# Projection and retention of a hybrid encoder layer in one stage of two passes

## The chip, the cores and the metric

The kernel runs on one core of a Trainium2 chip. The core has five engines with a queue each: PE (TensorE, matmuls and transposes), DVE (VectorE), ACT (ScalarE), POOL (GpSimd) and SP (SyncE, which here only issues transfers). They run side by side and wait for each other through semaphores. Matmul results go to PSUM, eight banks of 128 x 512 FP32; all else is in SBUF. The metric is the device time of one execution in microseconds (us).

## The reference

The input is 12 tiles of 128 tokens with 1024 columns, in two sequences of 4 and 8 tiles. The part that the change touches computes:

```python
h = _rmsnorm(x, g_mix)
proj = jnp.einsum('bsd,de->bse', h, w_in)            # 1024 -> 512+512+512+512+448
rq, rk, rv, rg, cq, ckv, kr = jnp.split(proj, cuts, axis=-1)
q = _apply_rope(rq...); k = _apply_rope(rk...) * (DK_RET ** -0.5); v = rv...
ret = _retention_bidir(q, k, v, ret_log_decay)       # 8 heads of 64, chunks of 128 tokens
mu = jnp.mean(ret, axis=-1, keepdims=True)
var = jnp.mean(jnp.square(ret - mu), axis=-1, keepdims=True)
ret = ((ret - mu) * lax.rsqrt(var + EPS)).reshape(...) * ret_gn_g
ret_out = jax.nn.silu(rg) * ret
```

Retention of a chunk is `(q k^T * dmat) v` within the chunk, plus `q` times a state that a scan over the chunks carries forward, plus `q` times one that it carries backward. So no chunk's output can be made before the keys and values of its whole sequence are there. Behind this come latent attention, the output projection, a router and 32 gated experts; the change leaves them alone.

## The kernel before

Five stages run one after the other, with a barrier between: `phase_project` (names a_), `phase_retention` (b_), `phase_latent` (c_), the output projection with the router (d_), and the experts (e_). All that the first stage makes goes through the scratch tensor `mid` in DRAM, 12 records of 128 x 3072.

FP32 precision in the large matmuls is had by splitting each operand into a high and a low part and adding three products (`three_passes`, L110 to L112, on tiles of type F32R). The small matmuls of retention are plain FP32; the profile records two instructions for each of them.

`phase_project` holds the whole of w_in, split, in SBUF (`w_hi`, `w_lo`). For each of the 12 tiles PE makes five products with it: C (latents, 448 columns), Q, K, V and G (512 each), each of 8 slices of the contracted dimension with three passes, so 24 matmuls. DVE rotates queries and keys (`rotate`), PE transposes C, Q and K through one bank (`transpose_out`, L248), ACT takes them out, and SP stores the record (L209). While tile t is projected PE also transposes x of tile t + 1 (L225), ACT takes its high part and DVE its low part.

`phase_retention` first loads keys and values of every tile (L484), weighs the values with both decays on DVE (L687), makes the chunk's states with 8 matmuls (L549) and copies them out. Then DVE runs the scan over all chunks. Then, for each tile, SP loads queries, keys, values and gates (L494, L495), PE makes scores (L562, 8 heads, odd and even heads in turn from the two halves of the partitions), products with the states (L572) and outputs (L584), DVE weighs and normalises, POOL multiplies by the gate, PE transposes (L598), ACT copies out, and POOL stores to `mixT` (L531).

`pairs` unrolls the first and the last two tiles and loops over those between.

Of the kernel before, what the change touches and what calls it, by code (L numbers as in the profile page):

```python
# [19 lines left out]
F32 = mybir.dt.float32  # L20
# [8 lines left out]
P = 128  # L29
D = 1024  # L30
# [13 lines left out]
M_QT, M_KT, M_K, M_V, M_G, M_CT = 0, 512, 1024, 1536, 2048, 2560  # L44
M_W = 3072
# [27 lines left out]
def phase_sems(nc, ctx):  # L73

    sems = []

    def clear():
        nc.clear_and_free_semaphores(sems)
        nc.all_engine_barrier()

    ctx.callback(clear)
    return sems


def phase_sem(nc, sems, name):
    sems.append(nc.alloc_semaphore(name))
    return sems[-1]


# [25 lines left out]
def phase_project(nc, x_all, w_in, g_mix, g_q, g_kv, rope, ident_d, mid):  # L115
    with ExitStack() as ctx:
# [8 lines left out]
        w_hi, w_lo = sb("w_hi", [P, KD, D_IN], F32R), sb("w_lo", [P, KD, D_IN], F32R)  # L125
        x_sb = sb("x_sb", [P, 2, D])
        xT_hi, xT_lo = sb("xT_hi", [P, 2, KD, P], F32R), sb("xT_lo", [P, 2, KD, P], F32R)
        rec = sb("rec", [P, M_W])
        rope_sb = sb("rope_sb", [P, 2, 2, DR])
        work = sb("work", [P, 4, 512])  # L130
        part1, part2, q_tok, c_tok = (work[:, i, :] for i in range(4))
        junk = sb("junk", [P, D], BF16)
        g_col = sb("g_col", [P, KD])
        gq_row, gkv_row = sb("gq_row", [P, QRANK]), sb("gkv_row", [P, KVRANK])
        ident = sb("ident", [P, P])
        eps = sb("eps", [P, 1])
        ssq = sb("ssq", [P, 3])
        root = sb("root", [P, 3])
        rstd = sb("rstd", [P, 3])

        stage = [rec[:, i * 1024:(i + 1) * 1024] for i in range(3)]
        stage += [work[:, 2 * i:2 * i + 2, :].rearrange("p a n -> p (a n)") for i in range(2)]
        NST = len(stage)

        pG = [ctx.enter_context(nc.psum_tensor(f"a_pG{g}", [P, 512], F32)) for g in range(5)]
        pX = [ctx.enter_context(nc.psum_tensor(f"a_pX{b}", [P, 512], F32)) for b in range(2)]
        pO = ctx.enter_context(nc.psum_tensor("a_pO", [P, 512], F32))
        C, Q, K, V, G = range(5)
        COLS = {Q: (0, RW), K: (RW, RW), V: (2 * RW, RW), G: (3 * RW, RW), C: (4 * RW, CW)}
        PARTS = KD // 2  # L150

        def part(m):

            c0, w = COLS[m // PARTS]
            k = 2 * (m % PARTS)
            return slice(k, k + 2), slice(c0, c0 + w), stage[m % NST][:, 0:2 * w].rearrange("p (k n) -> p k n", k=2)

        s_const = sem("const")
        s_raw = [sem(f"raw{i}") for i in range(NST)]
        s_whi, s_wlo = sem("whi"), sem("wlo")  # L160
        s_x = [sem("x0"), sem("x1")]
        s_sq = sem("sq")
        s_root, s_rstd = sem("root"), sem("rstd")
        s_croot = sem("croot")
        s_xt = sem("xt")
        s_hi, s_lo = sem("hi"), sem("lo")
        s_proj = sem("proj")
        s_ctok, s_qtok = sem("ctok"), sem("qtok")

        s_ev = {C: s_ctok, Q: s_qtok, K: sem("evk"), V: sem("evv"), G: sem("evg")}  # L170
        s_out = sem("out")
        s_outev = sem("outev")
        s_store = sem("store")
        s_dve = sem("dve")
        s_eps = sem("eps")
# [3 lines left out]
        @block.sync  # L179
        def _(sp):  # L180
            sp.dma_start(x_sb[:, 0, :], x_all[0]).then_inc(s_x[0], 16)
            sp.dma_start(rope_sb[:, 0], rope[0]).then_inc(s_x[0], 16)
            sp.dma_start(ident[:], ident_d).then_inc(s_const, 16)
            sp.dma_start(g_col[:], g_mix.rearrange("(p k) -> p k", k=KD)).then_inc(s_const, 16)
            sp.dma_start(gq_row[:], g_q.partition_broadcast(P)).then_inc(s_const, 16)
            sp.dma_start(gkv_row[:], g_kv.partition_broadcast(P)).then_inc(s_const, 16)
            w_v = w_in.rearrange("(p k) n -> p k n", k=KD)
            for m in range(5 * PARTS):
                k, cols, raw = part(m)
# [4 lines left out]
            def tile(r, half, last):  # L194
                t = 2 * r + half
                if not last:

                    sp.wait_ge(s_xt, 2 * t)
                    sp.wait_ge(s_sq, t)
                    sp.wait_ge(s_ev[K], t)  # L200
                    sp.wait_ge(s_const, 64)
                    sp.dma_start(x_sb[:, 1 - half, :], x_all[t + 1]).then_inc(s_x[1 - half], 16)
                    sp.dma_start(rope_sb[:, 1 - half], rope[t + 1]).then_inc(s_x[1 - half], 16)
                sp.wait_ge(s_outev, 3 * (t + 1))
                sp.wait_ge(s_ev[V], t + 1)
                sp.wait_ge(s_ev[G], t + 1)
                sp.wait_ge(s_ev[K], t + 1)
                sp.wait_ge(s_const, 64)
                sp.dma_start(mid[t], rec[:]).then_inc(s_store, 16)  # L209

            pairs(sp, TILES, tile)
            sp.wait_ge(s_store, 16 * TILES)

        @block.gpsimd
        def _(pool):
            nc.gpsimd.memset(eps[:], EPS).then_inc(s_eps, 1)

        @block.tensor
        def _(pe):
            def transpose_x(n, half):  # L220

                for b in range(2):
                    for j in range(4):
                        k = 4 * b + j
                        ins = pe.transpose(pX[b][:, j * P:(j + 1) * P], x_sb[:, half, k:D:KD], ident[:])  # L225
                    ins.then_inc(s_xt, 1)

            pe.wait_ge(s_const, 64)
            pe.wait_ge(s_x[0], 32)
            transpose_x(0, 0)  # L230

            def project(r, half, g, i):
                t = 2 * r + half
                first = isinstance(t, int) and t == 0
                pe.wait_ge(s_ev[g], t)
                c0, w = COLS[g]
                for k in range(KD):
                    if first and k % 2 == 0:
                        pe.wait_ge(s_wlo, i * PARTS + k // 2 + 1)
                    ins = three_passes(pe, pG[g][:, 0:w], xT_hi[:, half, k, :], xT_lo[:, half, k, :],  # L240
                                       w_hi[:, k, c0:c0 + w], w_lo[:, k, c0:c0 + w], k == 0, k == KD - 1)
                ins.then_inc(s_proj, 1)

            def transpose_out(r, half, i, src):
                t = 2 * r + half
                pe.wait_ge(s_outev, 3 * t + i)
                for j in range(4):
                    ins = pe.transpose(pO[:, j * P:(j + 1) * P], src[:, j * P:(j + 1) * P], ident[:])  # L248
                ins.then_inc(s_out, 1)

            def tile(r, half, last):
                t = 2 * r + half
                first = isinstance(t, int) and t == 0
                pe.wait_ge(s_lo, 2 * (t + 1))
                project(r, half, C, 0)
                project(r, half, Q, 1)
                if first:
                    project(r, half, K, 2)
                    project(r, half, V, 3)
                    project(r, half, G, 4)  # L260
                pe.wait_ge(s_ctok, t + 1)
                transpose_out(r, half, 0, c_tok)
                if not first:
                    project(r, half, K, 2)
                pe.wait_ge(s_qtok, t + 1)
                transpose_out(r, half, 1, q_tok)
                if not first:
                    project(r, half, V, 3)
                pe.wait_ge(s_ev[K], t + 1)
                transpose_out(r, half, 2, rec[:, M_K:M_K + RW])  # L270
                if not last:
                    pe.wait_ge(s_x[1 - half], 32 * (r + 1 + half))
                    transpose_x(t + 1, 1 - half)
                if not first:
                    project(r, half, G, 4)

            pairs(pe, TILES, tile)

        @block.scalar
        def _(act):  # L280
            def hi_of_x(n, half):
                for b in range(2):
                    act.wait_ge(s_xt, 2 * n + b + 1)
                    for j in range(4):
                        k = 4 * b + j
                        ins = nc.scalar.activation(xT_hi[:, half, k, :], pX[b][:, j * P:(j + 1) * P],
                                                   ACT.Copy, scale=g_col[:, k:k + 1])
                    ins.then_inc(s_hi, 1)
# [1771 lines left out]
```

## Time and profile before

| | us |
|---|---|
| median of 3 runs (lowest, highest) | 1807.42 (1805.31, 1809.92) |
| the profiled execution | 1802.13 |
| its span, first to last instruction | 1800.6 |
| busy PE, DVE, ACT, POOL in the span | 1494.7, 1078.9, 835.3, 358.4 |
| mean granted clock of TensorE | 0.908 |

A granted clock of 1.00 is 2.4 GHz and one of 0.50 is 1.2 GHz; a value between is a mix of both over the stretch. Busy PE means that a matmul was under way, at either clock. Start times count from the start of the span.

### The profile page before, as it was taken

Reading aid. Unit: us, or ns where it says so; the run is one execution under the profiler, and the core shown is the slowest. Engines: PE = TensorE matmul, PEld = TensorE weight load, DVE = VectorE, ACT = ScalarE, POOL = GpSimd, SP = SyncE. Lnnn points to the kernel's source line nnn. Section 1 sums busy time; section 2 is a strip of 40 time slices with the busy share of each in tenths; the row PEclk is TensorE's granted clock in tenths of the full one; section 3 lists DMA queues with packets and bytes.
Section 4 is the critical chain, followed back from the end, with each engine's and each line's share of the span. In section 5 each row is a group of like instructions: output and inputs, shape, how many; then the busy total and the mean of one; then the engine's idle time right before and its main releaser. Section 6 shows DMA issues by size and latency. Waiting matters only on the chain. (4 is left out here: it accounts for less than half of the span.)

```text
span 1800.6 us, 21880 instructions
## 1 busy us (share of the span) xinstructions
PE 1494.7 (83%) x7330; PEld 1224.4 (68%) x7330; DVE 1078.9 (60%) x1689; ACT 835.3 (46%) x1139; POOL 358.4 (20%) x327
## 2 busy tenths in 40 slices
PE   6799999954674779996699963999999999999990
PEld 5688888843673657885488852777777777777770
DVE  5322323224774656764345544888788887888784
ACT  5323232321564455543322213776667666766664
POOL 0000000000462000000011213233433433343330
PEclk9899999976675889999699976999999999999995
DMA  7121221224353110001633454999999999999977
GB/s 260 49 97 61 83 83 61 84 81 151 106 175 119 59 65 24 13 12 38 216 116 133 135 215 138 319 359 362 355 355 360 357 361 353 357 361 358 360 234 291
DMA packets 83585, 347.35 MB, mean 193 GB/s; under 512 B 14514, under 2 KB 25922, under 8 KB 57282
## 3 DMA queue, kind: packets, MB, share of 16 engines
q1 hardware_dynamic: 66434, 300.37, 45.6%
q0 software_dynamic: 17104, 46.38, 9.2%
q8 instruction: 26, 0.43, 0.1%
q14 instruction: 21, 0.17, 0.0%
HBM read 288.61 MB, written 63.87 MB: 196 GB/s over the span
## 5 line engine op out<-in xcount | busy, mean ns | idle before, releaser
L1923 DVE TENSOR_TENSOR e_w_lo<-raw,e_w_hi 128x2048 fp32r<-128x2048 f32 x192 | 430.8, 2285 | 40.9 <-ACT e_w_hi L1872 40.9
L1872 ACT CAST e_w_hi<-raw 128x2048 fp32r<-128x2048 f32 x192 | 353.8, 1921 | 0.0
L110 PE MATMUL a_pG<-a_w_hi,a_xT_hi 128*128 128x512 f32 (+1 forms) x480 | 189.8, 395 | 8.7 <-DVE a_w_lo L353 6.1
L112 PE MATMUL a_pG<-a_w_hi,a_xT_lo 128*128 128x512 f32 (+1 forms) x480 | 186.5, 388 | 0.0
L111 PE MATMUL a_pG<-a_w_lo,a_xT_hi 128*128 128x512 f32 (+1 forms) x480 | 186.1, 388 | 0.0
L1772 POOL DMA_INDIRECT e_xg<-s_h_rows,e_who x34 | 84.2, 2477 | 261.3 <-DMA e_who<-s_table 137.9
L110 PE MATMUL e_py<-e_w_hi,e_hT_hi 128*128 128x512 f32 x256 | 104.3, 408 | 30.4 <-DVE e_hT_lo L1955 30.4
L110 PEld LDWEIGHTS a_pG<-a_w_hi,a_xT_hi 128*128 128x128 f32 x480 | 91.2, 190 | 25.9 <-issue 5.5
L110 PE MATMUL e_pg<-e_w_hi,e_xT_hi 128*128 128x512 f32 x256 | 104.3, 408 | 4.9 <-DVE e_w_lo L1923 4.9
L110 PE MATMUL d_po<-d_w_hi,d_mT_hi 128*128 128x512 f32 x192 | 81.7, 426 | 26.0 <-DVE d_w_lo L1552 26.0
L112 PEld LDWEIGHTS a_pG<-a_w_hi,a_xT_lo 128*128 128x128 f32 x480 | 91.1, 190 | 17.2
L111 PEld LDWEIGHTS a_pG<-a_w_lo,a_xT_hi 128*128 128x128 f32 x480 | 91.3, 190 | 15.7
L111 PE MATMUL e_pg<-e_w_lo,e_xT_hi 128*128 128x512 f32 x256 | 101.8, 398 | 0.0
L112 PE MATMUL e_pg<-e_w_hi,e_xT_lo 128*128 128x512 f32 x256 | 101.7, 397 | 0.0
L112 PE MATMUL e_py<-e_w_hi,e_hT_lo 128*128 128x512 f32 x256 | 101.1, 395 | 0.0
L112 PE MATMUL e_pu<-e_w_hi,e_xT_lo 128*128 128x512 f32 x256 | 101.0, 395 | 0.0
L110 PE MATMUL e_pu<-e_w_hi,e_xT_hi 128*128 128x512 f32 x256 | 101.0, 395 | 0.0
L111 PE MATMUL e_pu<-e_w_lo,e_xT_hi 128*128 128x512 f32 x256 | 101.0, 394 | 0.0
L111 PE MATMUL e_py<-e_w_lo,e_hT_hi 128*128 128x512 f32 x256 | 101.0, 394 | 0.0
L1280 DVE TENSOR_TENSOR c_pT_lo<-c_pt,c_pT_hi 128x512 fp32r<-128x512 f32 x80 | 52.1, 684 | 46.8 <-ACT c_pT_hi L1131 46.8
L112 PE MATMUL d_po<-d_w_hi,d_mT_lo 128*128 128x512 f32 x192 | 79.9, 416 | 0.0
L111 PE MATMUL d_po<-d_w_lo,d_mT_hi 128*128 128x512 f32 x192 | 79.9, 416 | 0.0
(314 smaller groups left out, 3092.2 us busy)
## 6 DMA issues: line engine op xcount, KB each, us to landing
raw<-in_w_gate SPq DMA_DIRECT2D x64, 1024.0 KB, 6.6
raw<-in_w_up SPq DMA_DIRECT2D x64, 1024.0 KB, 9.6
raw<-in_w_down SPq DMA_DIRECT2D x64, 1024.0 KB, 8.2
s_mid<-a_rec SPq DMA_DIRECT2D x12, 1536.0 KB
a_x_sb<-in_x SPq DMA_DIRECT2D x12, 512.0 KB, 6.4
b_kv<-s_mid SPq DMA_DIRECT2D x12, 512.0 KB, 4.1
b_qk<-s_mid SPq DMA_DIRECT2D x12, 512.0 KB, 4.1
b_vg<-s_mid SPq DMA_DIRECT2D x12, 512.0 KB, 5.5
```

What stands on the lines that cost most here:

```text
L110: pe.matmul(out, st_hi, mv_hi, start=first, stop=False)
L111: pe.matmul(out, st_hi, mv_lo, start=False, stop=False)
L112: return pe.matmul(out, st_lo, mv_hi, start=False, stop=last)
L1280: nc.vector.tensor_tensor(pT3_lo[:, 4 * i:4 * i + 4, j * P:(j + 1) * P], pt[:, c * 512:(c + 1) * 512].rearrange("p (k i) -> p k i", k=4), ...
L1772: pool.indirect_dma_start(out=xg[half][:], out_offset=None, in_=h_rows, in_offset=bass.IndirectOffsetOnAxis(ap=who[half][:, 0:1], axis=0), ...
L1872: nc.scalar.copy(w_hi[:, j // 2, span(j)], raw[:, j // 2, span(j)]).then_inc(s_whi[j], 1)
L1923: nc.vector.tensor_tensor(w_lo[:, j // 2, span(j)], raw[:, j // 2, span(j)], w_hi[:, j // 2, span(j)].bitcast(F32), ALU.subtract).then_inc ...
```

## The change

`phase_retention` goes, and `phase_project` takes in its work, in two passes over the 12 tiles, without loops (every tile is written out).

Pass 1 makes values and keys. The values are centred over each head's 64 columns (so that the output's mean, which the group norm subtracts, is zero), the keys are rotated, transposed and weighed, and eight matmuls make the chunk's states (`own_state`). Both states of a head stand above each other on the partitions (`st`), and the scan is done step by step between the tiles. Transposed keys and values go to `mid` and come back in pass 2.

Pass 2 loads and transposes x again and makes queries, latents and gates. Between the projections of tile t stand the scores and outputs of tile t - 1 and the transposition of the output of tile t - 2. The queries of a head are written twice side by side, so that one matmul with `st` gives both directions, and it adds to the same bank as the product within the chunk. The weights need not all be in SBUF: three slots hold V, K and Q, and then C and G take the places of V and K. The norm's gain `g_mix` moves from x to the weights. Pieces of the weights are one slice (128 x 512) with six buffers; the first two groups come by SP's queue, the others by POOL's.

The core of the new order, PE's and ACT's:

```diff
+            for t in range(N):
+                pe.wait_ge(s_lo, 2 * (t + 1))
+                if t >= 2:
+                    pe.wait_ge(s_vev, t - 1)
+                project(V, t, pV[t % 2], low)
+                transpose_x(t + 1)
+                project(V, t, pV[t % 2], high).then_inc(s_pv, 1)
+                if t:
+                    own_state(t - 1)
+                if t >= 2:
+                    pe.wait_ge(s_krot, t - 1)
+                project(K, t, pK[t % 2], range(KD)).then_inc(s_pk, 1)
...
+                project(Q, n, pQ, range(KD)).then_inc(s_pq, 1)
+                if t:
+                    scores(t - 1, 0)
+                else:
+                    own_state(N - 1)
...
+                project(C, n, pC, low)
+                if t:
+                    scores(t - 1, 1)
+                project(C, n, pC, high).then_inc(s_pc, 1)
+                if t >= 2:
+                    turn(t - 2)
+                turn_queries(t, 0)
+                if t:
+                    outputs(t - 1)
+                if t + 1 < N:
+                    transpose_x(n + 1)
...
+                project(G, n, pG, low)
+                turn_queries(t, 1)
+                project(G, n, pG, high).then_inc(s_pg, 1)
+                turn_latent(t)
```

```diff
+                if t == 0:
+                    take_keys(N - 1)
+                    take_own(N - 1)
+                    for m in range(G * KD, (G + 1) * KD):
+                        split_w(m)
+                latent_norm(t)
+                if t >= 2:
+                    take_turned(t - 2)
+                take_queries(t, 0)
+                if t:
+                    square_out(t - 1)
+                if t + 1 < N:
+                    hi_of_x(N + t + 1)
+                if t:
+                    root_out(t - 1)
+                take_queries(t, 1)
+                take_gate(t)
+                take_latent(t)
```

```diff
+            def scores(t, odd):
+                rows = slice(odd * DR, (odd + 1) * DR)
+                for pair in range(HR // 2):
+                    cols = slice(pair * P, (pair + 1) * P)
+                    ins = pe.matmul(pS[:, cols], kv[rows, t % 2, cols], qd[rows, 2 * pair + odd, :],
+                                    start=True, stop=True)
+            def outputs(t):
+                for h in range(HR):
+                    out = pO[:, h * DR:(h + 1) * DR]
+                    pe.matmul(out, sc[:, h % 2, h // 2, :], kv[:, t % 2, 512 + h * DR:512 + (h + 1) * DR],
+                              start=True, stop=False)
+                    ins = pe.matmul(out, qs[:, h, :], st[:, t, h, :], start=False, stop=True)
```

ACT's queue before, in the first tile of projection: the latent norm's squares (L313, L315) and roots (L318, L319) and what follows them. `a_pO` is the bank of transposes.

```order
L313 ACTIVATE a_junk,a_ssq<-a_pG0,a_rstd 128x256 [waits a_proj,a_rstd]
L315 ACTIVATE a_junk,a_ssq<-a_pG0,a_rstd 128x128
L318 ACTIVATE a_root<-a_ssq,a_eps 128x1 [waits a_croot]
L319 ACTIVATE a_root<-a_ssq,a_eps 128x1
L301 COPY a_rec<-a_pO 128x512 [waits a_out,a_store]
L301 COPY a_rec<-a_pO 128x512 [waits a_out]
L325 ACTIVATE a_rec<-a_pG3,a_rstd 128x512 [waits a_proj]
```

ACT's queue after the change, in a middle tile of pass 2, from the gate of the tile before to the queries. `a_p6` is the bank of transposes, `a_p2` the latents' and `a_p1` the gates'; L600 is the gate's silu, L573 takes the turned output, L580 the turned queries.

```order
L600 ACTIVATE a_late<-a_p1,a_rstd 128x512 [waits a_pg]
L606 COPY a_ct<-a_p6 128x512 [waits a_cst,a_ct]
L559 ACTIVATE a_c_junk0,a_cssq<-a_p2,a_rstd 128x256 [waits a_cinv,a_pc]
L559 ACTIVATE a_c_junk1,a_cssq<-a_p2,a_rstd 128x128
L563 ACT_TABLE_LOAD
L563 ACTIVATE a_croot<-a_cssq,a_eps 128x1 [waits a_csq]
L564 ACTIVATE a_croot<-a_cssq,a_eps 128x1
L573 COPY a_late<-a_p6 128x512 [waits a_rst,a_rt]
L580 COPY a_qd<-a_p6 128x512 [waits a_qs,a_ps,a_qt]
```

A table load now stands between squares and roots, and the copy that empties the bank of transposes stands behind both.

PE's queue after the change, at the same place: the end of the latent projection (L93 to L95), the output of tile t - 2 turned (L401), the queries turned (L417), and the first outputs of tile t - 1.

```order
L94 MATMUL a_p2<-a_w_lo,a_xT_hi 128x448
L95 MATMUL a_p2<-a_w_hi,a_xT_lo 128x448
L401 MATMUL a_p6<-a_ident,a_late 128x128 [waits a_ctev,a_ret]
L401 MATMUL a_p6<-a_ident,a_late 128x128 x3
L417 MATMUL a_p6<-a_ident,a_tok 128x128 [waits a_rtev,a_qrot]
L417 MATMUL a_p6<-a_ident,a_tok 128x128 x3
L390 MATMUL a_p3<-a_kv,a_late 128x64 [waits a_scan,a_zero,a_nrm,a_qs,a_sc]
L392 MATMUL a_p3<-a_st,a_qs 128x64
```

L417 waits for `a_rtev`, which L573 of ACT gives; before, PE went from one transposition to the next with a whole projection between.

## Rows read from the trace of the kernel before

**Rows 1.** Windows by stage: window, length, busy us (instructions) of each engine, clock, DMA

```profile
60.00:380.00 320.00, 318.96 (x1530) 270.11 (x1528) 95.09 (x278) 82.63 (x231) 0.00 (x0) 0.99 0.20 72
380.00:460.00 80.00, 25.33 (x212) 20.91 (x214) 38.99 (x89) 13.73 (x33) 0.84 (x2) 0.57 0.39 131
460.00:562.50 102.50, 72.63 (x608) 66.76 (x604) 71.38 (x154) 60.90 (x82) 65.49 (x60) 0.72 0.39 134
```

**Rows 2.** Waits of PE, 380 to 563 us: total, times, longest

```profile
PE b_pst L549 <- DVE b_vw L687: 38.8, 11, 20.6
PE b_pin L572 <- ACT b_cur L631: 16.9, 1, 16.9
```

**Rows 3.** Timeline of PE, 354 to 368 us: start, duration, instruction

```profile
354.75 0.36 PE L112 MATMUL a_pG<-a_w_hi,a_xT_lo 128*128 128x448 f32 x1
...
355.36 0.36 PE L112 MATMUL a_pG<-a_w_hi,a_xT_lo 128*128 128x448 f32 x1
...
365.60 0.39 PE L110 MATMUL a_pG<-a_w_hi,a_xT_hi 128*128 128x512 f32 x1
...
366.74 0.39 PE L112 MATMUL a_pG<-a_w_hi,a_xT_lo 128*128 128x512 f32 x1
...
366.97 0.60 PE L248 MATMUL a_pO<-a_ident,a_work 128*128 128x128 f32 x4
...
367.63 0.39 PE L111 MATMUL a_pG<-a_w_lo,a_xT_hi 128*128 128x512 f32 x1
```

**Rows 4.** Timeline of SP, the first and last of nine stores in the loop

```profile
91.01 0.34 SPq L209 DMA_DIRECT2D s_mid<-a_rec  x1
...
322.92 0.36 SPq L209 DMA_DIRECT2D s_mid<-a_rec  x1
```

**Rows 5.** Timeline of PE in retention, at full and (last row) half clock

```profile
491.11 1.90 PE L584 MATMUL b_pno<-b_vg,b_sc 128*128 128x64 f32 x16
494.79 1.16 PE L562 MATMUL b_psc<-b_qk 64*128 64x128 f32 x16 [1.78 <-DMA b_vg<-s_mid]
495.79 1.06 PE L572 MATMUL b_pin<-b_cur,b_qk 64*128 64x128 f32 x16
...
544.49 3.26 PE L584 MATMUL b_pno<-b_vg,b_sc 128*128 128x64 f32 x16 [1.30 <-DVE b_sc L718]
```

**Rows 6.** Timeline of DVE: first and last of the four instructions of one rotation

```profile
361.24 0.75 DVE L364 SCALAR_TENSOR_TENSOR a_work<-a_pG,a_rstd,a_rope_sb 128x512 f32<-128x512 f32 x1 [1.70 <-PE a_pG L112]
...
362.80 0.69 DVE L371 TENSOR_TENSOR a_work<-a_work 128x512 f32<-128x512 f32 x1
```

**Rows 7.** Timeline of ACT: latent norm's first and last, and a table load

```profile
355.82 0.47 ACT L313 ACTIVATE a_junk<-a_pG,a_rstd 128x256 bf16<-128x256 f32 x1 [2.87 <-PE a_pG L112]
...
356.97 0.28 ACT L319 ACTIVATE a_root<-a_ssq,a_eps 128x1 f32<-128x1 f32 x1
...
544.39 1.28 ACT L651 ACT_TABLE_LOAD   x1
```

**Rows 8.** Timeline, 554 to 563 us: the end of retention

```profile
554.39 1.26 POOL L525 TENSOR_TENSOR b_ret<-b_nrm,b_gate 128x512 f32<-128x512 f32 x1
...
556.86 0.58 ACT L657 COPY b_retT<-b_ptr 128x512 f32<-128x512 f32 x1 [3.90 <-PE b_ptr L598]
...
562.68 1.45 SPq L842 DMA_DIRECT2D c_work<-s_mid  x3
```

**Rows 9.** Timeline of PE: the first transposes and the first projection matmul

```profile
8.30 1.97 PE L225 MATMUL a_pX<-a_ident,a_x_sb 128*128 128x128 f32 x8 [8.30 <-DMA a_gkv_row<-in_g_kv]
...
15.36 0.71 PE L110 MATMUL a_pG<-a_w_hi,a_xT_hi 128*128 128x448 f32 x1 [5.08 <-DVE a_w_lo L353]
```

**Rows 10.** Waits of PE (first row) and windows as in rows 1

```profile
PE a_pO L248 <- DVE a_work L395: 3.5, 1, 3.5
...
50.00:55.00 5.00, 2.28 (x10) 1.88 (x11) 3.67 (x7) 1.71 (x4) 0.00 (x0) 0.51 0.00 0
834.00:837.00 3.00, 1.17 (x8) 0.84 (x8) 2.93 (x7) 2.12 (x5) 0.00 (x0) 1.00 0.00 0
```

More of the change, by code:

```diff
@@ L150, in phase_project @@
[L150 to L159, printed above, removed]
+        xT_hi, xT_lo = sb("xT_hi", [P, 2, D], F32R), sb("xT_lo", [P, 2, D], F32R)
+        late = sb("late", [P, NST, 512])
+        st = sb("st", [P, N, HR, DR])
+        wqT = sb("wqT", [P, HR, P])
@@ new lines, in last_of, with first_of @@
+        def last_of(t):
+            return any(t == first + tiles - 1 for first, tiles in SEQS)
+        def first_of(t):
+            return any(t == first for first, _ in SEQS)
+        scan_steps = []
+        for first, tiles in SEQS:
+            for t in range(first, first + tiles):
+                if t > first and not last_of(t):
+                    scan_steps.append((t, slice(0, DR), t, t + 1))
+                if last_of(t):
+                    scan_steps += [(t, slice(DR, P), i + 1, i) for i in range(t - 2, first - 1, -1)]
@@ L177, in phase_project, with states_ready @@
+        TAIL = sum(1 for step in scan_steps if step[0] == N - 1)
+        def states_ready(t):
+            seq_end = next(first + tiles for first, tiles in SEQS if t < first + tiles)
+            return 2 * sum(1 for step in scan_steps if step[0] < seq_end)
         block = ctx.enter_context(nc.Block())
@@ L192, in _ @@
                 sp.dma_start(raw, w_v[:, k, cols]).then_inc(s_raw[m % NST], 16)
[L194 to L209, printed above, removed]
@@ L224, in transpose_x @@
                         k = 4 * b + j
-                        ins = pe.transpose(pX[b][:, j * P:(j + 1) * P], x_sb[:, half, k:D:KD], ident[:])
+                        ins = pe.transpose(pX[b][:, j * P:(j + 1) * P], x_sb[:, n % 2, k:D:KD], ident[:])
                     ins.then_inc(s_xt, 1)
[L228 to L242, printed above, removed]
@@ L279, in _, with hi_of_x @@
+            scores(N - 1, 0)
+            scores(N - 1, 1)
+            turn(N - 2)
+            outputs(N - 1)
+            turn(N - 1)
         @block.scalar
         def _(act):
-            def hi_of_x(n, half):
+            def hi_of_x(n):
                 for b in range(2):
                     act.wait_ge(s_xt, 2 * n + b + 1)
[L284 to L288, printed above, removed]
@@ new lines, in _ @@
+            for m in range(C * KD, (C + 1) * KD):
+                split_w(m)
+            for t in range(N):
+                if t == 0:
+                    turn_keys(N - 1)
+                    weigh_keys(N - 1)
+                    for m in range(G * KD, (G + 1) * KD):
+                        split_w(m)
+                else:
+                    decayed(t - 1, 0)
+                turn_queries(t)
+                if t:
+                    decayed(t - 1, 1)
+                latent(t)
+                weigh_queries(t, 0)
+                if t:
+                    spread(t - 1)
+                if t + 1 < N:
+                    lo_of_x(N + t + 1)
+                if t:
+                    normalise(t - 1)
+                weigh_queries(t, 1)
+                if t < TAIL // 2:
+                    scan(N - 1, t)
@@ L758 @@
+            decayed(N - 1, 0)
+            decayed(N - 1, 1)
+            spread(N - 1)
+            normalise(N - 1)
 W_QN, W_KT, W_VT, W_QR, W_CAT = 0, 1024, 1536, 2048, 2560
```

1056 lines of the change are left out of this document (570 added, 486 removed).

## Prediction

> **What bounds the kernel now.** I read the stages first. In the row for 60 to 380 us of [rows 1] PE is busy 318.96 of 320 us at a granted clock of 0.99: projection is bound by TensorE and nothing else. The two rows after it are retention: from 380 to 460 us PE is busy 25.33 of 80 us, from 460 to 562.5 us 72.63 of 102.5, at clocks 0.57 and 0.72. The waits in [rows 2] name why: PE stood 38.8 us waiting for the weighed values, and 16.9 us once, while the scan of states ran. So retention is 183 us in which TensorE has little to do, and every matmul in it is small. The change puts this work between projection matmuls. The question is what TensorE's own work costs per tile, and which new waits stand in it.
>
> **What a tile costs TensorE, from rows.** In [rows 3] five 512-column matmuls take 366.74 - 365.60 = 1.14 us, 0.228 each; three 448-column ones 0.61, 0.203 each; and between 366.74 and 367.63 stand two 512-column matmuls and four transposes, so a transpose costs (0.89 - 0.456)/4 = 0.11. Test: a projection tile of before is 24 x (4 x 0.228 + 0.203) + 20 x 0.11 = 28.96 us, and the stores in [rows 4] come every (322.92 - 91.01)/8 = 28.99. A group of eight FP32 matmuls with 128 x 128 weights and 64 columns takes 1.90 us at full clock and 3.26 at half, and the eight score matmuls 1.16, after 1.00 of which the next group starts [rows 5].
>
> **Pass 1, per tile.** Values and keys 48 x 0.228 = 10.9, 12 transposes 1.3, eight state matmuls 1.9 (the form of L584: 128 x 128 weights, 64 columns): 14.1 us. DVE has one rotation (363.49 - 361.24 = 2.25 us [rows 6]) and eight to ten operations of 0.69, about 9 us; ACT about 6. Both are covered. If a cover failed, the keys' rotation must be done 6.8 us after their projection, and it needs 2.3.
>
> **Pass 2, per tile.** Queries and gates 10.9, latents 24 x 0.203 = 4.9, 24 transposes 2.6, outputs 16 matmuls of L584's form 3.8. The scores now come as four of one row half and then four of the other, where before they alternated. Bounds: 1.0 as before, 1.9 as L584's; no row shows the grouped form, and I take the middle, 1.5. Together 23.7 us. The Trainium skill, TensorEngine Tiling (Array Packing), Key Properties, says that tiles in different row halves run in parallel, for up to 2x; by that rule grouping them loses it, the price would be 1.9 to 2.0, and the sum 5 to 6 us longer. DVE has some 12 us of work here, ACT some 9, POOL 3.
>
> **The new wait.** PSUM bank a_p6 takes all transposes. In the ACT order the copy that empties it of the retention output (L573) stands behind the latent norm (L559 to L564), which waits for the end of the latent projection and now has a table load in its middle. PE turns that output at once after the latent projection and then needs the bank again for the queries. From [rows 7]: first square to end of second root is 357.25 - 355.82 = 1.43 us, the table load is 1.28, the copy that follows 0.58 [rows 8], the semaphores 0.2: 3.5 us, less the 0.44 that PE uses for its four transposes. So PE stands 3.0 us in each of the ten tiles from the third on: 30 us of the gain go here. Behind PE's wait are the output matmuls, the next x transposes and the gates; nothing else is late, as the other engines have slack. The Trainium skill, ScalarE: Activation LUTs, gives about 2.7 us for a table load; the trace has 1.28 and that is used. By the page's figure the ten waits would be 14 us longer.
>
> **The rest of the path.** Start: the first transposes begin at 8.30 and the first projection matmul at 15.36 [rows 9]. ACT sets the end of tile 0: about 1.2 after the transposes begin a table load of 1.28, four x casts and sixteen weight pieces of 512 elements at 0.58 (11.6), two squares of 1024 elements with roots (at twice 0.58 and 0.3 each, 3), a second table load: 8.3 + 1.2 + 1.3 + 11.6 + 3 + 1.3 = 26.7, with DVE's last subtraction 27 us. A first tile of before needs all five weight groups, now two; that gain is inside the sum. Then eleven tiles of 14.1: 155. In the first of them the state matmuls wait for the decay tables: ACT comes to them behind two x casts (their transposes end at 27 + 2.7 + 0.9) and a square, at 33.3. Then come the table load, five exponentials of 8 columns and eight of 128 columns (between 0.2 and 0.4 each, so some 3.7) and DVE's two weighings of 0.69: 39.7. PE is ready at 27 + 5.5 + 0.9 + 0.4 = 33.8. That is 6 us, and 2 for matmuls at half clock behind so long a wait: 8 us. Tile 0 of pass 2: 15.8 of projection, 2.3 of states, 20 transposes 2.2, and a wait. The eight gate pieces are split only after ACT has taken the last state, 9 us into the tile; at 0.69 each on DVE they end at 15 at the earliest, and the last two, whose buffers come free only then, add a transfer (between nothing and 6 us; I take 3). Behind them on DVE is the queries' rotation, 2.9: 21 us, where PE is ready at 12.7. So 8 us, between 5 and 11. Sum 28.4. Tile 1 without the output's transposes: 23.3. Ten tiles of 26.7: 267. End: last scores and products 3, outputs 5 (between 3.8 and 6.5), square 0.6, table load 1.3, root, reciprocal and normalising 1.3: 3.2, and from POOL's last product to the first DMA of the latent stage 562.68 - 554.39 = 8.3 [rows 8]: 19.5. Together 27 + 155 + 8 + 28.4 + 23.3 + 267 + 19.5 = 528, where the trace of before has 562.7. That is 34 us less before the clock.
>
> **The clock.** Each wait of 3 us is followed by small matmuls. What this does to the granted clock no row decides: in [rows 10] it fell to 0.51 in 50 to 55 us after PE had stood 3.5 us, and it is 0.72 on average in retention [rows 1], but in 834 to 837 PE was busy 1.17 of 3 us and kept 1.00. One fall costs 2.7 us if it lasts over the outputs (2 x 3.26 - 2 x 1.90 [rows 5]). I take four falls in ten tiles, 11 us. So the stage ends at about 539 and the gain is 23 us. Later stages are not touched; they start earlier.
>
> The profiled execution took 1802.13 us; 1802.13 - 23 = 1779. It lies 5.3 under the median of the runs, 1807.42. Prediction: 1785 us.
>
> **The rivals.** (a) The clock holds in pass 2: then 34 us are kept, 1774; with scores at 1.0 and no wait for the decay tables, 1762. For it: 834 to 837. Against it: retention's own clock. (b) The weight pieces that now come by POOL's queue are late, at the change of passes and in the start, and cost 15 to 20 us more: 1800 to 1805. For it: six buffers of one piece, each refilled only after it is split; against it: the six first pieces of the latents lie ready long before. (c) The slower side: the clock falls in every tile of pass 2 and comes back only in the gates. Then the outputs cost 2.7 more, twelve transposes 1.3 (twice 0.11 each), and twelve of the gates' 24 matmuls, at twice 0.228, 2.7: 6.7 per tile, 67 in ten tiles against the 34 saved, 33 us slower than before, 1840. It decides from 3.4 us per tile on. (d) The change does not do what it says: the retention pieces are serial in each tile, because some engine's queue puts every tile's chain on the path. The queues speak against it: the chain of tile t is spread over tiles t + 1 and t + 2.
>
> **How the numbers follow.** Forecast (1775 to 1797) 0.45; clock holds (1760 to 1775) 0.25; late weights (1797 to 1812) 0.14; clock falls always, or serial chains (1812 to 1845) 0.16. What a measurement of this kernel can tell from no change is 0.3%, 5.4 us: 1802 to 1813. Faster 0.76, same 0.10, slower 0.14. The range of 8 in 10 runs from 1764 to 1815.
>
> **What would show it.** Right: steps of 14.1 us between values' projections in pass 1; a line of PE waiting for ACT's L573 ten times for about 3 us, the largest wait of the stage; the ACT table load before L563 in front of it; PE waiting once 6 us for the weighed keys and once about 8 us before the first queries' transposes; the latent stage's first DMA near 540 us. Wrong, if the pass 2 tiles are well under 26.7 us with a clock of 1.00 (wait or scores too dear), or above 29 (clock), or if PE's waits in pass 1 are more than that one.

## The result, and the profile after

| | before | after |
|---|---|---|
| median of 4 runs each (lowest, highest), us | 1808.13 (1805.31, 1809.92) | 1839.31 (1833.08, 1849.72) |
| the profiled execution | 1802.13 | 1849.72 |
| mean granted clock in it | 0.908 | 0.905 |
| first DMA of the latent stage in it | 562.68 [rows 8] | 599.20 |

The change makes the kernel slower: the ratio is 1.018, 95% interval 1.013 to 1.0229, so 31 us by the medians. The profiled execution of after is the longest of its four. Of its 47.6 us over the one of before, 36.5 are there when the latent stage begins. The other 11 lie in later stages, whose code is the same. (What is called the latent stage's first DMA here and in the prediction is its first load from `mid`, L985; a load of weights stands 0.4 us ahead of it, before and after.)

Windows by stage of the changed kernel, with the columns of [rows 1]: the start, pass 1, the change of passes, and most of pass 2.

```profile
0.00:60.00 60.00, 38.99 (x162) 32.19 (x163) 26.75 (x47) 27.30 (x53) 3.80 (x12) 0.89 0.53 174
60.00:190.00 130.00, 130.00 (x704) 111.51 (x703) 81.50 (x144) 54.21 (x101) 4.31 (x8) 1.00 0.27 88
190.00:250.00 60.00, 51.23 (x277) 44.14 (x277) 36.87 (x66) 24.55 (x47) 7.28 (x12) 0.94 0.32 109
250.00:500.00 250.00, 226.63 (x1123) 198.16 (x1121) 85.87 (x170) 67.33 (x131) 25.10 (x24) 0.85 0.15 49
```

Pass 1 is what it was meant to be: PE is busy all 130 us at full clock. In pass 2 PE is busy for 227 of 250 us, far more than in the old retention, but the clock is 0.85: for about 30% of the time the array ran at 1.2 GHz. Busy time hides this; only the clock column tells it.

The waits of PE in the stage, 0 to 600 us (total, times, longest), which answer to [rows 2]:

```profile
PE a_p L417 <- ACT a_late L573: 29.2, 10, 2.9
PE a_p L417 <- DVE a_tok L707: 8.1, 1, 8.1
PE a_p L333 <- DMA a_x_sb<-in_x: 7.6, 1, 7.6
PE a_p L358 <- DVE a_qs L725: 5.3, 2, 4.6
```

The first row is the new wait that the prediction named, ten times 2.9 us. The two old waits of 38.8 and 16.9 us are gone. The third row, PE waiting for x of the third tile, is one that the prediction did not have.

Timeline from 296 to 312 us in a middle tile of pass 2 (start, duration, instruction, idle time before it and what ended it). It answers to [rows 5] and [rows 7]:

```profile
296.28 0.60 PE L401 MATMUL a_p<-a_ident,a_late 128*128 128x128 f32 x4
296.48 0.47 ACT L559 ACTIVATE a_c_junk<-a_p,a_rstd 128x256 bf16<-128x256 f32 x1 [12.18 <-PE a_p L95]
...
297.41 1.28 ACT L563 ACT_TABLE_LOAD   x1
...
299.09 0.56 ACT L573 COPY a_late<-a_p 128x512 f32<-128x512 f32 x1
...
299.80 0.63 PE L417 MATMUL a_p<-a_ident,a_tok 128*128 128x128 f32 x4 [2.92 <-ACT a_late L573]
...
300.26 0.33 PE L390 MATMUL a_p<-a_kv,a_late 128*128 128x64 f32 x2
300.43 0.39 PE L392 MATMUL a_p<-a_st,a_qs 128*128 128x64 f32 x2
...
304.60 0.63 PE L390 MATMUL a_p<-a_kv,a_late 128*128 128x64 f32 x2
...
306.30 1.91 PE L333 MATMUL a_p<-a_ident,a_x_sb 128*128 128x128 f32 x8
...
308.44 0.63 PE L94 MATMUL a_p<-a_w_lo,a_xT_hi 128*128 128x512 f32 x1
...
311.82 0.39 PE L94 MATMUL a_p<-a_w_lo,a_xT_hi 128*128 128x512 f32 x1
```

Read it down the ACT rows first: squares, table load, copy. PE has its four transposes done at 296.88, and the next ones start at 299.80, released by that copy. The outputs follow. Their pairs take 0.33 to 0.39 us at first, and 0.63 or 0.64 from 301 us on; a dense matmul takes 0.63 there and 0.39 again at 311.8. The same stretch by windows (the number after the five engines is the clock):

```profile
298.00:300.00 2.00, 0.20 (x2) 0.23 (x3) 0.71 (x3) 1.64 (x4) 0.05 (x1) 1.00 0.00 0
300.00:302.00 2.00, 2.00 (x16) 2.00 (x15) 1.23 (x6) 0.59 (x1) 0.54 (x1) 0.75 0.34 131
302.00:304.00 2.00, 2.00 (x12) 2.00 (x11) 0.00 (x0) 0.00 (x0) 0.00 (x0) 0.50 0.00 0
...
308.00:310.00 2.00, 2.00 (x7) 1.61 (x6) 1.79 (x4) 0.79 (x2) 0.00 (x0) 0.50 0.59 231
310.00:312.00 2.00, 2.00 (x7) 1.58 (x7) 0.40 (x1) 0.00 (x0) 1.27 (x1) 0.69 0.00 0
```

Here the clock falls 1.2 us after the wait is over, while PE is busy without a gap, and stays at 0.50 for some 10 us, through the outputs, the x transposes and the first gates. All ten tiles have such a fall, and in nine it lasts 10 us (in the first 7). It does not always come at this point: in six tiles it comes 1.2 to 1.4 us after PE went on, and in the other four 0.6 us before, while PE still waits. The next tile is one of these. PE goes on at 332.35, its transposes take 1.08 us from the start where the tile above had 0.63, and the clock is under 1.00 before 332 (PE's columns alone):

```profile
332.35 1.08 PE L417 MATMUL a_p<-a_ident,a_tok 128*128 128x128 f32 x4 [2.92 <-ACT a_late L573]
...
328.00:332.00 4.00, 1.42 (x9) 0.97 0.00 0
332.00:336.00 4.00, 3.65 (x18) 0.50 0.17 66
```

SP's stores give the pace, as in [rows 4]: in pass 1 one per tile, and in pass 2 one per tile.

```profile
91.87 0.33 SPq L242 DMA_DIRECT2D s_mid<-a_kv  x1
...
190.48 0.33 SPq L242 DMA_DIRECT2D s_mid<-a_kv  x1
...
253.36 0.32 SPq L287 DMA_DIRECT2D s_mid<-a_ct  x1
...
511.41 0.32 SPq L287 DMA_DIRECT2D s_mid<-a_ct  x1
543.67 32.00 SPq L287 DMA_DIRECT2D s_mid<-a_ct  x2
```

The last row holds the last two stores together. Seven steps of pass 1 take (190.48 - 91.87)/7 = 14.09 us each; nine of pass 2 take (543.67 - 253.36)/9 = 32.3.

### The profile page after: what moved, and what is told of

The parts are those of the page before. It is cut to its first block and busy times, and to the rows that moved or that the text cites. A ratio compares the mean times of both kernels' runs of the same rounds, so it can differ in the third digit from the quotient of the medians.

```text
span 1848.2 us, 21620 instructions
## 1 busy us (share of the span) xinstructions
PE 1576.9 (85%) x7474; PEld 1300.3 (70%) x7474; DVE 1095.9 (59%) x1592; ACT 842.2 (46%) x1114; POOL 342.0 (19%) x325
## 5 line engine op out<-in xcount | busy, mean ns | idle before, releaser
L93 PE MATMUL a_p<-a_w_hi,a_xT_hi 128*128 128x512 f32 (+1 forms) x480 | 200.1, 417 | 4.1 <-DVE a_w_lo L672 4.1
L94 PE MATMUL a_p<-a_w_lo,a_xT_hi 128*128 128x512 f32 (+1 forms) x480 | 189.9, 396 | 0.0
L95 PE MATMUL a_p<-a_w_hi,a_xT_lo 128*128 128x512 f32 (+1 forms) x480 | 189.6, 395 | 0.0
L93 PE MATMUL e_py<-e_w_hi,e_hT_hi 128*128 128x512 f32 x256 | 104.4, 408 | 30.0 <-DVE e_hT_lo L2098 30.0
L93 PEld LDWEIGHTS a_p<-a_w_hi,a_xT_hi 128*128 128x128 f32 x480 | 94.7, 197 | 22.8 <-DVE a_xT_lo L666 3.7
L93 PE MATMUL e_pg<-e_w_hi,e_xT_hi 128*128 128x512 f32 x256 | 104.5, 408 | 4.9 <-DVE e_w_lo L2066 4.9
L95 PEld LDWEIGHTS a_p<-a_w_hi,a_xT_lo 128*128 128x128 f32 x480 | 93.4, 195 | 18.7
L93 PE MATMUL d_po<-d_w_hi,d_mT_hi 128*128 128x512 f32 x192 | 83.6, 435 | 25.7 <-DVE d_w_lo L1695 25.7
L94 PEld LDWEIGHTS a_p<-a_w_lo,a_xT_hi 128*128 128x128 f32 x480 | 94.6, 197 | 15.4
L95 PE MATMUL e_pg<-e_w_hi,e_xT_lo 128*128 128x512 f32 x256 | 101.9, 398 | 0.0
L95 PE MATMUL e_py<-e_w_hi,e_hT_lo 128*128 128x512 f32 x256 | 101.1, 395 | 0.0
L95 PE MATMUL e_pu<-e_w_hi,e_xT_lo 128*128 128x512 f32 x256 | 101.0, 395 | 0.0
L93 PE MATMUL e_pu<-e_w_hi,e_xT_hi 128*128 128x512 f32 x256 | 101.0, 394 | 0.0
L95 PE MATMUL d_po<-d_w_hi,d_mT_lo 128*128 128x512 f32 x192 | 81.4, 424 | 0.0
L93 PEld LDWEIGHTS e_py<-e_w_hi,e_hT_hi 128*128 128x128 f32 x256 | 48.1, 188 | 46.2 <-DVE e_hT_lo L2098 36.3
```

What stands on the lines that cost most here:

```text
L93: pe.matmul(out, st_hi, mv_hi, start=first, stop=False)
L94: pe.matmul(out, st_hi, mv_lo, start=False, stop=False)
L95: return pe.matmul(out, st_lo, mv_hi, start=False, stop=last)
```

## The experiments

Two theories stood against each other at first. W: the wait of 2.9 us, with small matmuls behind it, brings the clock down, and this is the loss. S: the small FP32 matmuls and transposes do it by themselves, with or without the wait. All kernels below are the changed one with an edit, unless said otherwise. "Tile" is the mean step of nine stores in pass 2, "stage" the first DMA of the latent stage in the profiled execution, "falls" the tiles of the ten (the third to the last) in which the clock falls at the wait or behind it, in the profiled execution, "ratio" that to the kernel before on the same chip. The medians are of four executions each, of ten in e3.

| kernel | median us | ratio (95%) | tile us | falls | clock, 250 to 500 us | stage us |
|---|---|---|---|---|---|---|
| after | 1839.31 | 1.018 (1.013 to 1.0229) | 32.3 | 10 | 0.85 | 599.20 |
| e1_turn_early | 1762.05 | 0.9756 (0.9733 to 0.9778) | 24.59 | 0 | 1.00 | 516.78 |
| e2_fill_wait | 1791.66 | 0.9924 (0.99 to 0.9947) | 27.75 | 0 | 1.00 | 550.35 |
| e3_outputs_late | 1806.58 | 1.0007 (0.9989 to 1.0026) | 28.5 | 5 | 0.97 | 556.69 |
| e4_x_first | 1834.88 | 1.0181 (1.0143 to 1.0218) | 31.4 | 9 | 0.88 | 584.62 |
| e5_table_early | 1790.87 | 0.9891 (0.9861 to 0.9922) | 27.7 | 3 | 0.95 | 551.25 |
| e12_short_late | 1781.33 | 0.9864 (0.9838 to 0.9891) | 26.44 | 0 | 1.00 | 539.08 |
| e8_all_fixes | 1754.78 | 0.97 (0.9674 to 0.9726) | 24.59 | 0 | 0.98 | 510.74 |
| e9_scores_in_turn | 1747.21 | 0.9666 (0.9636 to 0.9695) | 23.36 | 0 | 0.99 | 504.16 |
| e10_all | 1740.03 | 0.9614 (0.9586 to 0.9641) | 23.36 | 0 | 0.96 | 494.64 |
| e11_rope_split | 1739.69 | 0.9638 (0.9618 to 0.9657) | 23.36 | 0 | 0.97 | 495.51 |

(In the last four kernels 250 to 500 us reaches past pass 2 or close to its end, so that their clock there is a little under 1.00 for another reason.)

**The wait taken away (e1_turn_early).** PE turns the output of tile t - 2 one half of the latent projection earlier, and ACT takes it before the norm:

```diff
@@ PE @@
-                project(C, n, pC, high).then_inc(s_pc, 1)
                 if t >= 2:
                     turn(t - 2)
+                project(C, n, pC, high).then_inc(s_pc, 1)
@@ ACT @@
-                latent_norm(t)
                 if t >= 2:
                     take_turned(t - 2)
+                latent_norm(t)
```

> Only the order changes: PE turns the output of tile t - 2 before the last 12 matmuls of the latents, and ACT empties the bank of transposes ahead of the latent norm. Theory W (PE's wait of 2.9 us for L573, followed by small matmuls, is what lets the clock fall in each of ten tiles): wait and fall both go, a tile of pass 2 takes 24 to 25 us in place of 32.2, the clock stays at 1.00 there, time 1760 to 1770. Theory S (the stretch of small matmuls lets it fall by itself, with or without the wait): the wait goes, the fall stays, a tile takes about 29.3 us, time about 1810.

The time fell by 77 us against the changed kernel and is 2.4% under before. Window of 250 to 500 us, and ACT's two rows in a middle tile:

```profile
250.00:500.00 250.00, 249.02 (x1464) 215.53 (x1461) 111.23 (x217) 87.11 (x171) 33.74 (x32) 1.00 0.18 59
```

```profile
285.93 0.59 ACT L573 COPY a_late<-a_p 128x512 f32<-128x512 f32 x1 [10.13 <-PE a_p L401]
288.37 0.47 ACT L559 ACTIVATE a_c_junk<-a_p,a_rstd 128x256 bf16<-128x256 f32 x1 [1.85 <-PE a_p L95]
```

The copy now lies 2.4 us ahead of the squares, PE is busy 249 of 250 us, and the clock is 1.00 with the same outputs and transposes as before. So S is out: in this trace the small matmuls alone don't lower it. The wait was 2.9 us per tile, but taking it away gave 32.3 - 24.6 = 7.7.

**The wait filled (e2_fill_wait).** The wait's cause stays. In it PE makes 12 dense matmuls whose result nobody reads (the bank is overwritten by the outputs), so this kernel does more work and nothing sooner:

```diff
+            def filler(t, n):
+                pe.wait_ge(s_nrm, t - 1)
+                for k in range(4):
+                    three_passes(pe, pO[:], xT_hi[:, n % 2, rows], xT_lo[:, n % 2, rows],
+                                 w_hi[:, SLOT[Q], k, :], w_lo[:, SLOT[Q], k, :], k == 0, k == 3)
...
                     turn(t - 2)
+                if t >= 2:
+                    filler(t, n)
                 turn_queries(t, 0)
```

> The wait for L573 keeps its place and length, but 12 needless 512-column matmuls (2.7 us, into the outputs' bank, which the outputs then overwrite) run in it. Nothing else changes. Theory W: the clock holds and a tile takes about 28 us although it has more work, time about 1797 or less. Theory S: a tile stays at 32 to 33 us, time about 1839.

```profile
250.00:500.00 250.00, 248.40 (x1406) 211.53 (x1406) 95.60 (x195) 77.05 (x154) 29.05 (x28) 1.00 0.17 55
```

PE's wait is 0.2 us now, ten times. Useless work makes the kernel 48 us faster. That is the price of the falls alone, since the queries' transposes come as late as in the changed kernel: 32.3 - 27.75 = 4.5 us per tile. The other 27.75 - 24.59 = 3.2 is the wait itself.

**The outputs moved from behind the wait (e3_outputs_late).** The wait stays at 2.9 us ten times; behind it come twelve transposes and then dense matmuls, and the outputs stand behind the gates' low half (their ACT and DVE steps move with them).

```diff
                 turn_queries(t, 0)
-                if t:
-                    outputs(t - 1)
                 if t + 1 < N:
                     transpose_x(n + 1)
...
                 project(G, n, pG, low)
+                if t:
+                    outputs(t - 1)
                 turn_queries(t, 1)
```

> The wait for L573 stays at 2.9 us, but the 16 output matmuls move behind the first half of the gates, so that four transposes, eight transposes and then twelve 512-column matmuls follow the wait. If the wait alone lets the clock fall (a first form of W): a fall in each tile, 31 to 32 us per tile, time 1830 to 1840. If it takes the wait and the outputs together (a second form): clock 1.00, about 27.5 us per tile, time about 1792. Theory S without the wait's part: the outputs, now between dense matmuls, no longer lower it either, as in the second form; this run does not tell S from the second form, the first two do.

```profile
PE a_p L417 <- ACT a_late L573: 29.2, 10, 2.9
```

Of the nine steps five are 27.7 us, as in e2 with no fall, and four are 29.0 to 30.5. The tenth tile, which they don't hold, has a fall too. The same wait brings the clock down in five tiles of ten now, it stays down for 3 to 7 us and not for 10, and a fall costs 1.3 to 2.8 us where it cost 4.5. Two windows with a fall, around the tile in which PE goes on at 351.20, and in the last tile, where it goes on at 523.23:

```profile
350.00:355.00 5.00, 3.80 (x15) 3.61 (x16) 2.98 (x10) 2.80 (x7) 0.58 (x1) 0.53 0.14 52
524.00:528.00 4.00, 4.00 (x12) 3.12 (x11) 0.66 (x4) 0.48 (x1) 0.00 (x0) 0.57 0.17 66
```

A mean of 0.53 over the first window means that the clock was down from 350.3, in the wait; so it is in one more of the five. In the last tile it falls 1.1 us after PE went on, among dense matmuls. So with the outputs moved the falls are fewer, shorter and cheaper, but neither the wait alone settles whether the clock falls, as W had it in its plain form, nor what follows it.

**The wait shortened (e5_table_early).** The table load, 1.28 of the 2.9 us, is moved out of the norm by a root of a constant at the end of the tile before:

```diff
                 take_latent(t)
+                if t + 1 < N:
+                    nc.scalar.activation(early_root[:, t:t + 1], eps[:], ACT.Sqrt, bias=eps[:, 0:1], scale=1.0)
```

> The changed kernel, with one ACT instruction more per tile of the second pass: a root of a constant into a scratch column, at the end of the tile's ACT work, so that the table load of 1.28 us comes there and no longer between the square and the root of the latent norm. TensorE's wait for L573 should shrink from 2.9 to about 1.6 us; small matmuls still follow it. If the fall of the clock needs a wait near 3 us, it is gone and a tile takes 25.9 to 26.3 us: ten tiles are 60 us shorter, the time is about 1776 to 1780. If any wait ahead of the small matmuls brings it down, only 1.3 us per tile are gained: 30.9 us per tile and about 1826.

Neither: the wait is 1.6 us ten times, and the clock fell in three tiles (steps of 31.3, 29.7 and 29.7 us against 26.5). This profiled execution, at 1798.86 us, is the longest of its four.

**Both partial remedies (e12_short_late).** The diffs of e3 and e5 together:

```diff
                 project(G, n, pG, low)
+                if t:
+                    outputs(t - 1)
...
                 take_latent(t)
+                if t + 1 < N:
+                    nc.scalar.activation(early_root[:, t:t + 1], eps[:], ACT.Sqrt, bias=eps[:, 0:1], scale=1.0)
```

> The changed kernel with both partial remedies: the outputs behind the gates' correction pass (e3), so that dense matmuls follow the wait, and the table load out of the latent norm (e5), so that the wait is 1.6 us and not 2.9. The clock fell in 10 of 10 tiles with neither, in 4 with the first and in 3 with the second. If length of the wait and what follows it both count, it falls in none or one: 26.4 us per tile, latent stage's first DMA at 538 to 543, about 1780. If falls come by chance at any wait, three or four again: first DMA at 546 to 552 and about 1789.

```profile
PE a_p L418 <- ACT a_late L574: 16.4, 10, 1.6
```

All nine steps are 26.44 us; no fall. The four kernels make a square, of falls in ten tiles:

| | outputs right behind the wait | outputs later |
|---|---|---|
| wait 2.9 us | 10 | 5 |
| wait 1.6 us | 3 | 0 |

(The text of e12 counts four in e3; with the last tile they are five.) Each count is that of one execution. Other executions of the same kernel can have another: e3's ten lie between 1801.88 and 1812.14 us, and its profiled one, at 1803.22, has the highest mean clock of them. The medians, 1839, 1807, 1791 and 1781 us, put the four in the same order. So both the length of the wait and the place of the outputs count. How the place acts isn't shown: four of the ten falls in the changed kernel and two of the five in e3 came before PE had gone on, so nothing that followed can have set them off. The falls in the mixed corners also say that whether one tile falls isn't settled by these two alone.

**The wait on x (e4_x_first).** In the changed kernel x of tile 2 stands on SP's queue behind the tables and gain rows. Here it stands ahead of them:

```diff
+            load_x(2)
             sp.dma_start(rope_sb[:].rearrange("p t a d -> p t (a d)"),
...
             for n in range(N):
-                load_x(n + 2)
+                if n:
+                    load_x(n + 2)
```

> Only SP's order at the start changes: x of the third tile is asked for before the tables and not behind them (PE waited 7.6 us for it, and the clock fell there). If that wait was on the path: 5 to 8 us faster, 1832 to 1834. If the wait for the weighed keys behind it (4.6 us), which hangs on the decay tables that are now asked for later, only grows by as much: no change, 1839.

```profile
PE a_p L353 <- DVE a_tok L707: 4.6, 1, 4.6
PE a_p L360 <- DVE a_qs L727: 2.0, 2, 1.4
```

The wait of 7.6 us on x is gone, and the first tile's rotated keys are late by 4.6 us instead, as their table now lands later. The store of pass 2's first tile comes 6 us sooner (223.07 against 229.14 us). The median is 4.4 us lower, which these intervals can't tell from nothing. The 14.6 us in the column "stage" are no measure of it: they compare the fastest of e4's four executions with the slowest of the changed kernel's.

**Three orders of the start on top of e1 (e8_all_fixes).**

```diff
+            load_x(2)
...
+            sp.dma_start(spans, span_d).then_inc(s_tabs, 16)
+            sp.dma_start(dist, dist_d).then_inc(s_tabs, 16)
+            sp.dma_start(rope_sb[:].rearrange("p t a d -> p t (a d)"),
+                         rope.rearrange("t p a d -> p t (a d)")).then_inc(s_const, 16)
@@ ACT, tile 1 of pass 1: ahead of the x casts @@
+                if t == 1:
+                    tables()
@@ ACT, tile 0 of pass 2: ahead of take_keys @@
+                    for m in range(G * KD, G * KD + 6):
+                        split_w(m)
```

> The kernel with the output turned before the latent projection (e1), and three orders more: x of tile 2 goes to SP's queue ahead of the tables, the decay tables are made on ACT ahead of the x casts of tile 1, and six of the eight gate pieces are split ahead of the last keys on ACT. If the waits on x (7.6 us), the weighed keys (4.6) and the first queries' transposes (8.1) are each worth what they show, 10 to 18 us go: 1744 to 1752. If they only uncover the next late thing (the weight pieces of the gates), less than 5 us go: 1757 or more.

```profile
PE a_p L354 <- DVE a_tok L710: 5.9, 1, 5.9
...
PE a_p L420 <- DVE a_tok L712: 3.3, 1, 3.3
...
PE a_p L361 <- DVE a_qs L730: 0.9, 2, 0.5
```

In e1 the three waits were 6.5 (x), 8.0 (first queries) and 4.3 us (weighed keys). Here they are 0, 3.3 and 0.9, but 5.9 for the keys' rotation is new. So the stage is 6.0 us shorter, a third of the 18.8 that the three waits showed, and the median 7.3.

**The scores in turn (e9_scores_in_turn).** On top of e1, one group of eight scores alternates the row halves again, each half into a PSUM bank of its own:

```diff
-            def scores(t, odd):
...
-                rows = slice(odd * DR, (odd + 1) * DR)
-                for pair in range(HR // 2):
-                    cols = slice(pair * P, (pair + 1) * P)
-                    ins = pe.matmul(pS[:, cols], kv[rows, t % 2, cols], qd[rows, 2 * pair + odd, :],
+            def scores(t):
...
+                for h in range(HR):
+                    pair, odd = h // 2, h % 2
+                    rows, cols = slice(odd * DR, (odd + 1) * DR), slice(pair * P, (pair + 1) * P)
+                    ins = pe.matmul((pS, pG)[odd][:, cols], kv[rows, t % 2, cols], qd[rows, h, :],
                                     start=True, stop=True)
```

> The kernel with the output turned before the latent projection (e1), and the eight score matmuls of a tile in one group that alternates the two row halves again, each half into a PSUM bank of its own. If the two groups of one half each cost 2.4 us of TensorE and the alternating one 1.0 to 1.2, a tile falls from 24.6 to about 23.3 us and the time by 14 to 16 us, to about 1747. If it is not the row halves that make the groups dear, the time stays at 1760 to 1762.

PE's timeline around one group of four in the changed kernel, and around the eight here (start and duration):

```profile
288.62 0.39 PE L95 MATMUL a_p<-a_w_hi,a_xT_lo 128*128 128x512 f32 x1
288.94 1.16 PE L375 MATMUL a_p<-a_qd,a_kv 64*128 64x128 f32 x8
...
290.34 0.36 PE L94 MATMUL a_p<-a_w_lo,a_xT_hi 128*128 128x448 f32 x1
```

```profile
302.76 0.39 PE L95 MATMUL a_p<-a_w_hi,a_xT_lo 128*128 128x512 f32 x1
303.07 1.16 PE L373 MATMUL a_p<-a_qd,a_kv 64*128 64x128 f32 x16
...
304.48 0.36 PE L94 MATMUL a_p<-a_w_lo,a_xT_hi 128*128 128x448 f32 x1
```

From the dense matmul ahead to the second one behind are 1.72 us in both. Less two dense matmuls (0.228 + 0.203) that is 1.3 us for four matmuls of one row half, and 1.3 for eight in turn. The tile goes from 24.59 to 23.36 us. The Trainium skill, TensorEngine Tiling (Array Packing), Key Properties, says that different tiles run in parallel. The trace agrees: eight in turn cost no more than four of one half, and grouping the heads by half, as the change did, gave that up. In both kernels that alternate the halves, before and e9, each half also has a PSUM bank of its own, so that the runs don't tell whether the halves alone would do.

**All of it (e10_all), and the rotation table in two pieces (e11_rope_split).** The first is e8 and e9 together; the second adds this:

```diff
+            sp.dma_start(rope_sb[:, 0:2].rearrange("p t a d -> p t (a d)"), rope_v[:, 0:2]).then_inc(s_const, 16)
             load_x(2)
...
+            sp.dma_start(rope_sb[:, 2:N].rearrange("p t a d -> p t (a d)"), rope_v[:, 2:N]).then_inc(s_rope, 16)
```

> Both of the two: all the orders of e8 and the alternating scores of e9. If the gains lie at different places of the stage they add up: 1728 to 1738. If either gives nothing, the time is that of the other.

> The kernel with all orders and the alternating scores (e10). In its trace TensorE waits 6.8 us for the rotated keys of the first tile, since the rotation table, moved behind x of tile 2, now lands after them: the wait on x went and this one came. Here the table's part for the first two tiles (a sixth of its bytes) is loaded ahead of x, the rest behind. If that wait is then worth what it shows, 4 to 6 us go: 1734 to 1736, and the latent stage's first DMA comes at 488 to 490 instead of 494.6. If the start of the stage is bound by the sum of its transfers, the wait only moves to x or the weights and less than 2 us go.

PE's waits in e11 (in e10 the same three were 3.1, 6.8 and 0.9 us):

```profile
PE a_p L420 <- DVE a_tok L712: 6.1, 1, 6.1
...
PE a_p L355 <- DVE a_tok L710: 4.0, 2, 3.8
...
PE a_p L362 <- DVE a_qs L730: 2.3, 2, 1.6
```

The gains of e8 and e9 over e1 add up: by the medians 7.3 and 14.8 us, and 22.0 for both. In the stage e8's orders give 504.16 - 494.64 = 9.5 us on top of e9, where they gave 6.0 on top of e1. The split table gives nothing: the wait for the first keys shrank by 2.8 us and the two others grew by 4.4 together. e10 is 3.9% faster than the kernel before, and some 100 us faster than the changed one; both keep its two passes.

## Why the prediction was wrong

**What held.** The pass 1 tile is 14.09 us against 14.1. The wait for ACT's L573 is 29.2 us in ten tiles against 30, with the table load in front of it. The first queries' wait is 8.1 against 8, the weighed keys' 4.6 against 6. Late weights (b) cost no more than the sum had for them: inside the 8.1 us ACT waits 3.7 us for the last two gate pieces from POOL's queue, and PE's own waits for weights are 3.3 and 0.7 us, both in the first tile. The chains aren't serial (d): without the wait PE is busy 249 of 250 us (e1).

**The step that failed** is the clock's: "I take four falls in ten tiles, 11 us." There were ten, and each cost 4.5 us (e2), where I took 2.7 "if it lasts over the outputs". It lasts over the outputs (300.26 to 306.30 us, 6.0 against 3.5 in e1, so 2.5), the x transposes and seven of the gates' matmuls, 10 us at half clock. Measured 45 us against 11, 34 too little. This alone turns 23 us of gain into a loss. The slower rival (c) had the mechanism: a fall in every tile that lasts into the gates. That its time, 1840, is also the measured one is luck, since it had 6.7 us a fall, 22 us too much in ten tiles, and none of the 26 us lost elsewhere. Its chance, 0.16 together with serial chains, was the mistake. The row with which I argued against it, PE busy 1.17 of 3 us and clock 1.00 [rows 10], was not the same case. In that stretch PE's longest wait is 1.99 us, and transposes alone stand behind it:

```profile
835.76 1.17 PE L989 MATMUL c_pt<-c_ident,c_work 128*128 128x128 f32 x8 [1.99 <-DVE c_pT_lo L1280]
```

The other row, 0.51 after a wait of 3.5 us, was the near one. And a wait that every tile repeats gives the clock the same occasion every time; to take four of ten for it had no row behind it, though e3's five and e5's three show that such numbers exist. The Trainium skill, TensorE: Matmul & The Clock Gate, HAM oscillation, describes a kernel whose clock falls in every tile because every tile waits, there for a DMA and for 3 to 5 us. The trace agrees on the repetition, ten of ten, and has it at waits of 2.9 us. I hadn't brought it in.

**The scores** were mis-sized. I took 1.5 us for the eight, with bounds of 1.0 and 1.9; they cost two times 1.3. That is 1.0 to 1.1 per tile, 11 to 12 us, and outside the bounds: L584's matmuls, from which the upper one came, have half the columns (64 against 128). With it the tile without a fall is 27.7 and not 26.7.

**The start** lacked a term. I counted SP's queue for the weights and not for x: 7.6 us of waiting, by which pass 1 ended at about 197 us and not 190. Tile 0 of pass 2 took 31 us against 28.4; the clock was at 0.50 for 7 us of it, which the sum did not have.

**The end** took 25 us from the last tile's last matmuls to the first DMA against 19.5. It ran at half clock too: the outputs took 7.0 us where I had 5, POOL's last product to the DMA 10.5 against the 8.3 of [rows 8], and the last scores with what stands behind them 4.1 against 3.

Together 34 + 11 + 7 + 3 + 5 = 60 us, and the stage ended at 599 against a forecast of 539. Two of the prediction's own signs of being wrong came: pass 2 tiles above 29 us, and a wait of PE in pass 1 that it did not name.

**What the change is worth** without its flaws of order is in e10: the stage ends at 494.64 instead of 562.68, 68 us sooner. The forecast before the clock, 528, was too early by itself: e2, in which the bank comes as late and the clock falls in none of the ten tiles, ends at 550, and e12, with a wait of 1.6 us and no fall in the ten, at 539. The scores, the start and the end are what 528 lacked.

## What to carry to other kernels

When work is moved between dense matmuls, price each new wait of TensorE twice: its own length, and half of the work that runs at half clock behind it. The second can be the larger (4.5 against 3.2 us here), and it comes in every tile that repeats the wait. First look for an order in which the copy that frees the bank stands ahead of anything long on its engine. If none is to be had, put dense matmuls behind the wait, shorten it, or even fill it. Keep small matmuls of 64 rows alternating between the row halves. Read the clock column beside the busy column: PE at 91% busy was a third slower per tile than it had to be.

## What the runs showed of the hardware

- The clock fell at waits of only 1.6 us three times of ten when four transposes and the outputs followed (e5), and not once at the same wait with twelve transposes and then dense matmuls behind (e12). At 2.9 us it fell in ten (after) and in five of ten (e3). All are counts of one execution each.
- The fall can come in the wait or behind it: in the changed kernel 0.6 us before PE went on in four tiles, and 1.2 to 1.4 us after in six. It then stayed at 0.50 for 10 us in nine of the ten tiles, while PE was busy throughout.
- The same outputs and transposes with no wait ahead keep 1.00 (e1); 12 needless dense matmuls per tile, 2.7 us, bring 4.5 us back (e2).
- Eight FP32 matmuls of 64 rows in alternating row halves cost TensorE 1.3 us, and four of one half the same. Whether that takes two PSUM banks as well stays open.
- What makes a single tile fall in the mixed cases, 5 and 3 of 10, stays open; so does why the split rotation table (e11) made the first queries later.
